# Differential attention's scores in three fp32r passes of split queries and keys, with weight remainders written over the raw weights

## What is computed

```
q = rmsnorm(q.reshape(b, t, 4, 2, 64), q_gain) * 64 ** -0.5
k = rmsnorm(k.reshape(b, t, 4, 2, 64), k_gain)
s = einsum('bqhcd,bkhcd->bhcqk', q_blk, k)          # c: the two maps of a head, d: 64
p = softmax(where(mask, s, neg))
wts = p[:, :, 0] - lam * p[:, :, 1]
o = einsum('bhqk,bkhv->bqhv', wts, v)
```

## Time and profile before

| what | us |
|---|---|
| median of three runs | 1082.01 (1078.73 to 1083.92) |
| the profiled execution | 1080.94 |
| its span in the profile | 1079.3 |
| TensorE matmul busy | 1016.9 |
| TensorE weight load busy | 799.7 |
| DVE busy | 637.0 |
| ACT busy | 296.3 |
| POOL busy | 72.3 |

### The profile page before, as it was taken

The page is one execution under the profiler, slowest core; times in us unless marked ns, Lnnn a source line. Parts: engine busy times, 40 slices in busy tenths (PEclk is TensorE's granted clock), DMA queues, the critical chain, the costliest instruction groups (busy, mean ns, idle before and its releaser), DMA issues.

```text
span 1079.3 us, 13803 instructions
## 1 busy us (share of the span) xinstructions
PE 1016.9 (94%) x4854; PEld 799.7 (74%) x4854; DVE 637.0 (59%) x1128; ACT 296.3 (27%) x534; POOL 72.3 (7%) x140
## 2 busy tenths in 40 slices
PE   5999999879999999999999998989999969999998
PEld 4876655558777777777788887777888857787887
DVE  5235765535567666666543434768778788634543
ACT  4132343413222222222111103643222325502220
POOL 1000000000000000000000000000000000000000
PEclk9999999989999999999999999989999979999999
DMA  9853322044445555555556553435432200113343
GB/s 316 258 183 130 113 94 87 1 156 156 160 172 175 195 175 175 190 179 175 196 176 213 176 182 131 156 138 174 145 129 98 98 1 1 39 47 125 123 143 111
DMA packets 35440, 153.52 MB, mean 142 GB/s; under 512 B 3904, under 2 KB 4672, under 8 KB 26944
## 3 DMA queue, kind: packets, MB, share of 16 engines
q0 software_dynamic: 19584, 71.31, 20.4%
q1 hardware_dynamic: 12384, 75.50, 19.6%
q10 hardware_dynamic: 3424, 6.04, 1.7%
HBM read 148.64 MB, written 4.19 MB: 142 GB/s over the span
## 4 chain that ended last, share of the span: by engine, by line
PE 58%; DVE 22%; ACT 8%; issue 7%; DMA 3%; DVEq 1%; ACTq 0%; POOLq 0%
PE bank L498 42%; DVE LO L1459 4%; DMA HI<-wstream 3%; ACT YC L1086 3%; DVE YC L1466 3%; DVE AB L1462 2%; DVE YC L1470 2%; PE bank L785 2%; DVE YC L1475 1%; DVE LO L1324 1%; PE bank L612 1%; ACT AH L1092 1%; PE bank L793 1%; PE bank L551 1%; PE bank L631 1%
## 5 line engine op out<-in xcount | busy, mean ns | idle before, releaser
L498 PE MATMUL bank<-GH,HI 128*128 128x512 f32 x720 | 295.3, 410 | 17.2 <-DVE AB L1462 8.7
L498 PE MATMUL bank<-GH,LO 128*128 128x512 f32 x720 | 282.4, 392 | 0.0
L498 PE MATMUL bank<-GL,HI 128*128 128x512 f32 x720 | 282.2, 392 | 0.0
L1324 DVE TENSOR_TENSOR LO<-RAW,HI 128x1024 fp32r<-128x1024 f32 x92 | 112.2, 1221 | 150.7 <-DMA HI<-wstream 141.8
L498 PEld LDWEIGHTS bank<-GH,HI 128*128 128x128 f32 x720 | 136.2, 189 | 60.4 <-DVE AB L1462 17.3
L498 PEld LDWEIGHTS bank<-GH,LO 128*128 128x128 f32 x720 | 135.7, 188 | 29.9
L498 PEld LDWEIGHTS bank<-GL,HI 128*128 128x128 f32 x720 | 136.3, 189 | 24.0
L486 POOL DMA_DIRECT2D HI<-wstream x132 | 69.9, 529 | 981.9 <-PE bank L498 972.0
L1086 ACT ACTIVATE YC<-AB,PAR 128x512 f32<-128x512 f32 x44 | 35.9, 816 | 145.5 <-DVE AB L1462 145.5
L498 PE MATMUL bank<-AH,HI 128*128 128x512 f32 x176 | 70.3, 400 | 0.4 <-DVE AB L1462 0.4
L498 PE MATMUL bank<-AH,LO 128*128 128x512 f32 x176 | 69.3, 394 | 0.0
(11 more groups left out here) (274 smaller groups left out, 1435.7 us busy)
## 6 DMA issues: line engine op xcount, KB each, us to landing
HI<-wstream POOLq DMA_DIRECT2D x136, 512.0 KB, 3.9
RAW<-wstream SPq DMA_DIRECT2D x66, 1024.0 KB, 4.8
X<-x_t SPq DMA_DIRECT2D x8, 256.0 KB, 13.3
RAW<-wstream SPq DMA_DIRECT2D x4, 512.0 KB, 13.0
out_t<-X ACTq DMA_DIRECT2D x8, 256.0 KB, 2.3
XR<-out_t ACTq DMA_DIRECT2D x8, 256.0 KB, 2.7
out_t<-XR SPq DMA_DIRECT2D x8, 256.0 KB, 2.4
CON<-consts ACTq DMA_DIRECT2D x1, 704.0 KB, 6.1
```

The costliest lines, as they stand in the source:

```text
L498: mm = pe.matmul(out, a, b, start=(first and n == 0), stop=(last and n == 2))
L1324: dve.tensor_tensor(LO[:, u % RING, :], RAW[:, u % RING, :], HI[:, u % RING, :].bitcast(F32), ALU.subtract).then_inc(unit_split, 1)
```

## The change

1. `LO` no longer has memory of its own: it is placed on `RAW`, and DVE writes the remainders over the raw weights that it reads in the same instruction.
2. SP therefore may load RAW of a slot only when TensorE is done with the slot. It now issues one load of 512 KB for each unit on `unit_done`, which is the condition and the moment at which POOL issues HI for the same slot. Before, it issued one load of 1024 KB for two units on `unit_split`. The six semaphores for landed RAW data become four.
3. The 16 KB per partition that this frees go to high parts of queries and keys, `DQH` and `DKH`. ACT writes them (part 3 of dfqk, after `qn_made`), eight copies of 128 x 512. DVE writes the low parts over `DQ` and `DK` (`low_qk`, eight subtractions of 128 x 512): that of tile n-2 in part 1 of step n, ahead of the ring step that follows part 1, and that of the last tile at the end of step 8.
4. `df_scores` waits for all eight splits and issues six fp32r products for each pair in place of two float32 ones: for each of the three passes map 0, then map 1. The waits for `dexp` stay ahead of the first pass of each map.

The diff, cut to its core:

```diff
-        RAW = place("RAW", [P, RING, 1024], F32)
+        RAW_AT = here[0]
+        RAW = place("RAW", [P, RING, 1024], F32)
+        LO = place("LO", [P, RING, 1024], F32R, RAW_AT)
         HI = place("HI", [P, RING, 1024], F32R)
-        LO = place("LO", [P, RING, 1024], F32R)
...
+        DQH = place("DQH", [P, 4, T], F32R, SPARE)
+        DKH = place("DKH", [P, 4, T], F32R, SPARE + 8 * KB)
+        DQL = place("DQL", [P, 4, T], F32R, arena + 72 * KB)
+        DKL = place("DKL", [P, 4, T], F32R, arena + 80 * KB)
...
-                for s in range(2):
-                    sp.wait_ge(unit_split, 4 * i + (2 * s - 2))
-                    sp.dma_start(RAW[:, 2 * s:2 * s + 2, :],
-                                 wstream[bass.ds(2 * i + s, 1)].rearrange("o p (a n) -> p (o a) n", a=2))\
-                      .then_inc(w_landed[s], 16)
+                for s in range(RING):
+                    sp.wait_ge(unit_done, 4 * i + (s - RING + 1))
+                    sp.dma_start(RAW[:, s, :],
+                                 wstream[bass.ds(2 * i + s // 2, 1), :, 1024 * (s % 2):1024 * (s % 2 + 1)]
+                                 .rearrange("o p n -> p (o n)")).then_inc(w_landed[s], 16)
...
-                pe.wait_ge(qn_made, 8)
-                for c in range(2):
-                    if n:
-                        pe.wait_ge(dexp, 2 * n + c - 1)
-                    pe.matmul(PS[c][:, 0:P * (i + 1)], DQ[64 * c:64 * c + 64, h, blk(i)],
-                              DK[64 * c:64 * c + 64, h, 0:P * (i + 1)], start=True, stop=True)\
-                      .then_inc(ds_mm, 1)
+                pe.wait_ge(qk_split, 8)
+                for part, (q, k) in enumerate(((DQH, DKH), (DQH, DKL), (DQL, DKH))):
+                    for c in range(2):
+                        if n and part == 0:
+                            pe.wait_ge(dexp, 2 * n + c - 1)
+                        r = slice(64 * c, 64 * c + 64)
+                        mm = pe.matmul(PS[c][:, 0:P * (i + 1)], q[r, h, blk(i)], k[r, h, 0:P * (i + 1)],
+                                       start=(part == 0), stop=(part == 2))
+                        if part == 2:
+                            mm.then_inc(ds_mm, 1)
...
+                    elif part == 3:
+                        act.wait_ge(qn_made, m + 1)
+                        act.activation((DQH if m % 2 == 0 else DKH)[:, m // 2, :],
+                                       (DQ if m % 2 == 0 else DK)[:, m // 2, :], ACT.Copy).then_inc(qk_high, 1)
...
+            def low_qk(m):
+                high, tile, low = ((DQH, DQ, DQL), (DKH, DK, DKL))[m % 2]
+                dve.wait_ge(qk_high, m + 1)
+                dve.wait_ge(qn_made, m + 1)
+                dve.tensor_tensor(low[:, m // 2, :], tile[:, m // 2, :], high[:, m // 2, :].bitcast(F32),
+                                  ALU.subtract).then_inc(qk_split, 1)
...
+                    if n >= 2 and part == 1:
+                        low_qk(n - 2)
                     if n >= 1 and part == 3:
                         normalise_qk(n - 1)
+                    if n == 8 and part == 3:
+                        low_qk(7)
```

More of the change, by code:

```diff
@@ L332, in build @@
         ST = place("ST", [P, 4, P], F32, arena + 98 * KB)
+        SPARE = arena + 100 * KB + 96
+        DQH = place("DQH", [P, 4, T], F32R, SPARE)
+        DKH = place("DKH", [P, 4, T], F32R, SPARE + 8 * KB)
+        DQL = place("DQL", [P, 4, T], F32R, arena + 72 * KB)
+        DKL = place("DKL", [P, 4, T], F32R, arena + 80 * KB)
+        assert SPARE + 16 * KB <= 229368, arena
         QNR = place("QNR", [P, T], F32, X_AT)
@@ L380, in build @@
         sg_landed = sem("sg_landed")
-        first_landed = [sem(f"first_landed{u}") for u in range(RING)]
-        w_landed = [sem("w_landed0"), sem("w_landed1")]
+        w_landed = [sem(f"w_landed{s}") for s in range(RING)]
         hi_landed = [sem(f"hi_landed{s}") for s in range(RING)]
@@ L422, in build @@
         qn_sq, qn_mm, qn_rt, qn_rc, qn_made = (sem(n) for n in ("qn_sq", "qn_mm", "qn_rt", "qn_rc", "qn_made"))
+        qk_high, qk_split = sem("qk_high"), sem("qk_split")
         tk_mm, tv_mm, g_mm, aq_mm = (sem(n) for n in ("tk_mm", "tv_mm", "g_mm", "aq_mm"))
@@ L461, in _ @@
                 sp.dma_start(RAW[:, u, :], wstream[u // 2, :, 1024 * (u % 2):1024 * (u % 2 + 1)])\
-                  .then_inc(first_landed[u], 16)
+                  .then_inc(w_landed[u], 16)
                 load_x(2 * u + 1)
@@ L1319, in ring_low @@
                 dve.wait_ge(hi_landed[u % RING], 16 * (u // RING + 1))
-                if u < RING:
-                    dve.wait_ge(first_landed[u], 16)
-                else:
-                    dve.wait_ge(w_landed[u % RING // 2], 16 * (u // RING))
+                dve.wait_ge(w_landed[u % RING], 16 * (u // RING + 1))
                 dve.tensor_tensor(LO[:, u % RING, :], RAW[:, u % RING, :], HI[:, u % RING, :].bitcast(F32),
@@ L1457, in _ @@
                         dve.wait_ge(hi_landed[slot], 16 * i + 16 * (turn + 1))
-                        dve.wait_ge(w_landed[slot // 2], 16 * i + 16 * turn)
+                        dve.wait_ge(w_landed[slot], 16 * i + 16 * (turn + 1))
                         dve.tensor_tensor(LO[:, slot, :], RAW[:, slot, :], HI[:, slot, :].bitcast(F32),
```

## The result

The changed kernel takes 1092.09 us (median of five runs, 1086.99 to 1093.68), the kernel before 1078.73 us in the runs beside it. The ratio is 1.0095, interval [1.0072, 1.0118]: slower by some 10 us, beyond the 0.5% that can be told from no change. The forecast was 1083.5 us with a range up to 1090. In the experiments the kernel before ran 61 more times, with a mean of 1080.0 us, so that 1078.73 is on the low side of it; against the mean of the five, 1091.1, the difference is 11 us.

What follows compares the result with a forecast made beforehand. TensorE, busy 94% of the span, plus its few waits was taken as the bound. The profiled 1080.94 - 0.8 + 2.0 + 0.25 gave 1082.4 us, and 1.1 to the median made 1083.5; range 1079 to 1090 us.

Steps and rivals of the forecast that it cites:

- Part 2: Splitting queries and keys: hidden until 849.6 us, then delaying the first scores; +2.0 us, bounds +1.4 and +3.4.
- Part 1: Differential scores: three fp32r passes against one float32 product, gaining in pairs 5 to 15; -0.8 us, bounds -1.5 and +4.5.
- rivals of no overlap: Scores: the two maps' fp32r passes run in turn, 4.6 us more than before, 1088.9 us; chance 0.10.
- narrow passes at float32's price: Scores: fp32r passes of 256 and 128 columns cost as much as float32 ones, 1086.9 us; chance 0.08.
- rival of a busier DVE between 784 and 860: Added subtractions and later `ring_low` bring DVE to TensorE's pace: 0.6 us in seven units, +4.2, 1087.7 us; chance 0.12.
- Part 3: RAW loads issued together with HI: HI lands after 4.6 us; sum over exposed landings +0.25 us, bounds -2.5 and +4.
- 8.0 us of cover: Feed-forward: HI asked for at 399.10 us is read at 407.09, so even a 5.72 us landing costs nothing.
- list of five: HI landings the prediction priced: 113.17 (+1.15 us), 230.03 (0), 644.68 (-1.1), 661.94 (+1.2), 725.39 (-1.0).
- only the landings in the chain count: Weight loads: only HI landings in the chain that ended last change the time; five were priced, +0.25 us together.
- 1.1 us for each unit without company: Weight loads: cost if every unit were exposed to HI and RAW sharing bandwidth; the prediction counted only five exposed landings.
- rival of the clock: At 868 to 885 us, longer idle time keeps the lower clock 5 us more: 1.8 us, 1085.3 us; chance 0.10.

Runs made afterwards that it cites:

- experiments 9: Changed kernel with HI copied from RAW by GpSimd everywhere but in the feed-forward, not fetched: 1085.99 us, ratio 1.0042 to the kernel before.
- experiment 10: Changed kernel with the three fp32r passes of one map issued before those of the other: 1090.66 us, ratio 1.0088 to the kernel before.
- experiment 1: Changed kernel with its weights side alone: scores as before, no splitting of queries and keys: 1091.7 us, ratio 1.0129 to the kernel before.
- experiment 5: Kernel before with RAW loaded one 512 KB unit at a time, issued on `unit_done`; LO keeps its own buffer: 1091.38 us, ratio 1.0122.
- experiment 6: Kernel before with RAW by the unit, issued on `unit_split`, and every HI copied from RAW by GpSimd, not fetched: 1081.19 us, ratio 1.0013.
- experiment 8: Kernel before with HI copied from RAW by GpSimd everywhere but in the feed-forward, where it is still fetched: 1068.88 us, ratio 0.9897.

## Why the prediction was wrong, and where it was right

**The scores side held.** Part 2 was +2.0 us: +2.1 up to the first score, and the wait grew from 3.13 to 4.45 us in all kernels with the splits, 1.3 for a forecast of 1.4. Part 1 was -0.8 us. The stage as a whole says little: from the first to the last score it takes 63.2, 63.9 and 64.0 us in the changed kernel and experiments 9 and 10, and 63.8 to 64.8 in the six kernels of the table that have no passes. The pairs say more. From the first record of a pair to TensorE's next instruction of another kind, the pairs 5 to 15 take 10.2 us before and 9.4 in the changed kernel, 0.8 us less, as forecast. One pair of 512 columns before, with the instruction behind it, and a narrow and a wide pair of the changed kernel:

```profile
900.36 1.13 PE L854 MATMUL bank<-DK,DQ 64*128 64x512 f32 x4
901.42 0.38 PE L793 MATMUL bank<-YM,XT 128*128 128x128 f32 x1
```

```profile
892.58 0.33 PE L864 MATMUL bank<-DKH,DQH 64*128 64x128 f32 x2
892.75 0.27 PE L864 MATMUL bank<-DKL,DQH 64*128 64x128 f32 x2
892.86 0.28 PE L864 MATMUL bank<-DKH,DQL 64*128 64x128 f32 x2
...
905.58 0.50 PE L864 MATMUL bank<-DKH,DQH 64*128 64x512 f32 x2
905.91 0.39 PE L864 MATMUL bank<-DKL,DQH 64*128 64x512 f32 x2
906.14 0.40 PE L864 MATMUL bank<-DKH,DQL 64*128 64x512 f32 x2
906.47 1.16 PE L801 MATMUL bank<-YM,XT 128*128 128x128 f32 x8
```

By these rows the wide pair takes 1.06 us before and 0.89 now, 0.17 less, as forecast. From the second pass to the third it is 0.23 us at 512 columns and 0.11 at 128, and both maps stand in each x2. That ends the rivals of no overlap and of narrow passes at float32's price. On the first base the ratios of the changed kernel and of experiment 1 (1.0095 and 1.0129) would make the scores side a gain of 3.7 us; their intervals are too wide to hold that against the rest.

**The rival of a busier DVE between 784 and 860** came with a fraction of its price: VectorE is busy 53.6 us from 784 to 850 in both profiles, and the changed kernel loses about 1 us there where it was to lose 4.2. The landings at 802.45 and 831.19 in its chain lie in that stretch, and experiments 1 and 5, which have no splits, lose 0.8 and 0.5 us there, so that most of it belongs to the landings.

**The landings failed: the term of Part 3.** It was +0.25 us, with bounds of -2.5 and +4. By their ratios experiments 1 and 5 put it at +14 and +13. Place by place, from the profile pair (a lag is the difference between the moments at which GpSimd takes up the same unit in the two kernels):
- 113.17: priced at +1.15. The lag grew by 1.1 us up to 145.37 and by 0.4 more up to 159.75. Right.
- 230.03: priced at 0. The lag did not change. Right.
- 274.82, the entry of the feed-forward, priced at nothing: +2.2 us. It stood in the chain of before with 4.88 us, and the prediction passed over it. Two units end within 0.7 us there, so that four copies start at once, and HI took 7.1 us. The prediction's worst price was 5.72 us, for one HI beside 1024 KB. The 8.0 us of cover are right for the turns behind the entry, and those lost nothing.
- 644.68: priced at -1.1. The gap fell by 0.8 us, but the time was not kept: at 655.72 the changed kernel has a wait of 0.56 us on VectorE that before has not, and at the next unit the lag is 2.2 us, against 2.0 ahead of the gap.
- 661.94: priced at +1.2. Two HI, the same pattern as at the entry, 6.2 and 6.9 us; a loss of 0.3 us at once in this profile.
- 690 to 700: not in the list of five, since no landing near it was in the chain of before. TensorE waits there for LO in both kernels (1.19 us before, 1.80 after, timeline), and 0.9 us stay.
- 725.39: priced at -1.0. HI landed 0.55 us sooner after its issue (5.56 and 5.01), but the lag stayed at 3.4 us: nothing was gained.
- 1034.28: +1.2 us. The prediction read the chain only up to 960 us, but reading on would not have helped: from 1015 to 1050 us the chain of before holds TensorE's work alone. The remainder of that unit stood ahead of the two QT instructions on VectorE there too, and was in time with a landing of 3.49 us; with 4.77 us it was not.

The step that failed is "only the landings in the chain count", and it failed in two ways. The list was read short: of the six landings in its own windows it left out 274.82, which lost more than any other landing in the profile pair. And the chain names what was latest in one execution, at one set of delays. Between the two profiles HI came later after its issue by 1.05 us in the median of 132 units (later by 1 us or more in 74, earlier in 20), and places that had been second latest came into the chain, as those at 802, 831 and 1034 us did. That the slack had to be asked for stood on the page of before:

```profile
L1324 DVE TENSOR_TENSOR LO<-RAW,HI 128x1024 fp32r<-128x1024 f32 x92 | 112.2, 1221 | 150.7 <-DMA HI<-wstream 141.8
```

VectorE waits for HI ahead of these 92 subtractions for 141.8 us in all, so a later landing makes most remainders later by as much, and only what lies behind them can absorb it.

Unit by unit, the kernel of experiment 5 falls behind before by 1.5 us from 122 to 160, by 2.2 at the entry of the feed-forward, by 2.4 from 645 to 662, by 3.3 from 662 to 718, by 0.4 from 809 to 846 and by 1.5 from 1029 to 1047 us, and makes 2.0 us good elsewhere. Those six stretches hold the loss of its profile (it began 1.0 us ahead and ended 8.4 behind). Those at the entry and from 645 to 662 us begin at landings that the chain of before lists; the two from 645 to 718 us hold some of the lower clock as well, which is told further below.

The sentences that should have weighed more stand beside each other in the prediction: that of the Trainium skill (DMA: Bandwidth & Descriptors, Issuing engines are not separate DMA queues), that issuing both loads at once brings no bandwidth, and the estimate from the rows behind it, 1.1 us for each unit without company. The trace agrees with the page in that the two loads share what there is: HI's median landing went from 3.9 to 4.9 us. It doesn't bear out that nothing is gained: HI alone moved 154 GB/s and took 3.44 us, and HI and RAW together moved 213 GB/s and took 5.0 us, not twice 3.44.

Some of the range was luck. On the 1078.73 us of the runs beside it the ratio gives 1089.0 us, just under the range's upper end of 1090. But that end was drawn for halves that do not overlap, which did not come, and no term for the landings reached so far; 1092.09 us lies outside. "Same" within 0.5%, which had 0.71, did not come: the interval begins at 1.0072.

**The profile pair is kinder than the times.** It shows 6.0 us where the means differ by 11. In 61 runs of the kernel before, time goes with the mean granted clock, 0.78 us for each 0.001 of it. That is a correlation: a wait lengthens the run and can bring the lower level with it. The changed kernel's profiled run had 0.983 and took 1086.99; its others had 0.978 to 0.981 and took 1089.9 to 1093.7. At 0.983 the kernel before takes 1078.2 us (mean of 15), so that the loss at that clock is 9 us, from one run of the changed kernel; between the means, 1091.1 us at 0.980 and 1080.0 us at 0.981, the clock is 0.7 of the 11 us. The profiled execution of before, in turn, was slow for its clock (0.982, at which the mean is 1078.5 and not 1080.94); where, its trace alone can't tell.

**Which stage carries it.** In experiments 1 and 5, which have no splits, the stretch from the down projection to the first score is 8 us longer than before. Windows over it (last three: granted clock, DMA share, GB/s), of the kernel before and of experiment 5:

```profile
651.60:867.20 215.60, 204.10 (x1097) 171.01 (x1097) 156.34 (x240) 76.71 (x109) 13.23 (x25) 0.98 0.38 130
```

```profile
652.00:875.20 223.20, 210.17 (x1099) 174.68 (x1099) 156.24 (x240) 76.72 (x109) 13.21 (x25) 0.95 0.39 128
```

The clock is 0.95 there, not 0.98, and TensorE takes 6 us more for the same matmuls. The lower level is held for 20.5 us between 600 and 800, not 10.2, each time from a wait on: 10.2 us of it after the wait before 652.78, where before had 3.4 us. At 0.78 us for 0.001, or an estimated 0.36 us for each us at the lower level, that is 3.7 of the 8 us. But in these two runs the first block had 7 us less of it than before (6.8, not 13.7), so over the whole span the clock is not what was lost; it is where within the span the loss shows. Why one wait of 2.4 us is followed by 10 us at the lower clock and one of 3.5 us by 3 was not settled. The prediction's rival of the clock, placed at 868 to 885, did not come: 3.4 and 10.2 us at the lower level in both.

## What to carry to other kernels

- Where many transfers get later, list every landing that the chain holds, and then count every place whose slack is less than the shift, in the chain or not; and price the place where several are issued at once by all their bytes.
- A prefetch that is far ahead of its use is worth its buffer. Here 16 KB were bought by moving RAW's load from the subtraction to the end of the unit, and that one wait cost 12 us.
- Ask whether the second fetch is needed at all. The raw weights lay in SBUF; rounding them by a copy on an idle engine, outside the stage where that engine's neighbour is tight, gave the fastest kernel of the study. Inside that stage the same copy gave the gain back (experiment 6).

## What the runs showed of the hardware

- From issue to landing, HI of 512 KB took 3.3 to 4.1 us where nothing of the stream ran beside it (53 units of before, 3.8 in the median), 4.9 in the median beside one RAW of 512 KB (104 units of the changed kernel), 5.7 and 5.6 beside one of 1024 KB at 644.68 and 725.39, and 6.2 to 7.7 where two HI and two RAW started within 1.5 us of each other (four HI of the changed kernel). Such stretches moved 154, 213, 276 and 272 to 323 GB/s.
- GpSimd's rounding copy of 128x1024 took 1.14 us in the mean of 88 (experiment 8), less than VectorE's subtraction of that size (1.22), and 1.54 us when it began beside a multiply-add of VectorE (experiment 6, at 411.15).
- Matmuls on the two halves of the rows start together (10 ns apart at 912.40 in experiment 10) even where three passes of one half are issued ahead of the first of the other; behind a wait they started 0.37 us apart and ran beside each other's later passes.
